# Down products of the feed-forward halves in three column blocks instead of two

## The reference

```
def swiglu(x, wi, wo):
    gate, up = jnp.split(x @ wi, 2, axis=-1)
    return (jax.nn.silu(gate) * up) @ wo
...
h = h + 0.5 * swiglu(rms_norm(h, ffn1_norm[li]), ffn1_wi[li], ffn1_wo[li])
```

## Time and profile before

| | |
|---|---|
| median of 3 runs | 1460.78 us |
| lowest and highest run | 1460.72 and 1460.96 us |
| profiled execution: span from the first to the last instruction | 1458.9 us |
| median of the runs less that span | 1.9 us |
| TensorE busy | 1452.6 us, 7822 matmuls |
| VectorE, ScalarE busy | 1002.6 and 778.5 us |

### The profile page before, as it was taken

The page is one execution under the profiler, slowest core; times in us unless marked ns, Lnnn a source line. Parts: engine busy times, 40 slices in busy tenths (PEclk is TensorE's granted clock), DMA queues, the critical chain, the costliest instruction groups (busy, mean ns, idle before and its releaser), DMA issues.

```text
span 1458.9 us, 18627 instructions
## 1 busy us (share of the span) xinstructions
PE 1452.6 (100%) x7822; PEld 1250.3 (86%) x7822; DVE 1002.6 (69%) x1216; ACT 778.5 (53%) x971; POOL 87.2 (6%) x113
## 2 busy tenths in 40 slices
PE   9999999999999999999999999999999999999999
PEld 7888888888888888888888888888888888888887
DVE  6976466787755867459877664787646987687653
ACT  6654355655534555345665544564435876465542
POOL 0000003000000000006100000000000800000000
PEclk9999999999999999999999999999999999999999
DMA  9855563556556555545455556475556543556552
GB/s 328 277 183 178 160 203 116 168 180 201 179 182 202 187 187 189 186 139 172 150 198 188 189 172 206 154 223 182 187 173 217 188 144 118 173 193 205 178 187 72
DMA packets 205620, 266.82 MB, mean 183 GB/s; under 512 B 6944, under 2 KB 148880, under 8 KB 205280
## 3 DMA queue, kind: packets, MB, share of 16 engines
q1 hardware_dynamic: 204320, 261.23, 54.5%
q0 software_dynamic: 1072, 4.35, 0.8%
q10 hardware_dynamic: 144, 0.05, 0.0%
HBM read 264.56 MB, written 1.05 MB: 182 GB/s over the span
## 4 chain that ended last, share of the span: by engine, by line
PE 96%; DVE 2%; ACT 1%; DMA 0%; issue 0%; DVEq 0%; ACTq 0%
PE ps L637 33%; PE ps L643 17%; PE ps L563 14%; PE ps L565 13%; PE ps L564 13%; PE ps L616 1%; PE ps L717 1%; PE ps L812 1%; DVE wlo L1632 1%; PE ps L750 1%; DVE d_i L2025 0%; DVE d_m L2021 0%; DMA G<-in_gains 0%; DVE d_i L2049 0%; PE ps L751 0%
## 5 line engine op out<-in xcount | busy, mean ns | idle before, releaser
L1632 DVE TENSOR_TENSOR wlo<-raw,whi 128x2048 fp32r<-128x2048 f32 (+5 forms) x275 | 567.4, 2068 | 259.0 <-ACT whi L1193 258.6
L1193 ACT CAST whi<-raw 128x2048 fp32r<-128x2048 f32 (+5 forms) x275 | 474.7, 1732 | 222.8 <-PE ps L565 218.4
L637 PE MATMUL ps<-xt,whi 128*128 128x512 f32 x2112 | 511.2, 391 | 0.5 <-DVE xt L2225 0.5
L637 PEld LDWEIGHTS ps<-xt,whi 128*128 128x128 f32 x2112 | 386.0, 188 | 74.4 <-DVE xt L2225 1.3
L643 PEld LDWEIGHTS ps<-xt,wlo 128*128 128x128 f32 x2112 | 274.0, 191 | 12.3
L643 PE MATMUL ps<-xt,wlo 128*128 128x256 f32 x2112 | 277.7, 283 | 0.0
L563 PE MATMUL ps<-whi,xt 128*128 128x512 f32 (+4 forms) x304 | 112.7, 371 | 0.0
L565 PE MATMUL ps<-whi,xt 128*128 128x512 f32 (+4 forms) x304 | 109.7, 361 | 0.0
L564 PE MATMUL ps<-wlo,xt 128*128 128x512 f32 (+4 forms) x304 | 109.5, 360 | 0.0
L563 PEld LDWEIGHTS ps<-whi,xt 128*128 128x128 f32 x304 | 57.3, 188 | 9.2 <-issue 1.0
L565 PEld LDWEIGHTS ps<-whi,xt 128*128 128x128 f32 x304 | 57.2, 188 | 8.5
(11 more groups left out here) (422 smaller groups left out, 1885.8 us busy)
## 6 DMA issues: line engine op xcount, KB each, us to landing
raw<-in_ffn_wi SPq DMA_DIRECT2D x85, 1024.0 KB, 4.9
raw<-in_ffn_wo SPq DMA_DIRECT2D x40, 1024.0 KB, 5.0
raw<-in_ffn_w_gate SPq DMA_DIRECT2D x22, 1024.0 KB, 5.1
raw<-in_ffn_w_up SPq DMA_DIRECT2D x22, 1024.0 KB, 5.2
raw<-in_ffn_w_down SPq DMA_DIRECT2D x20, 1024.0 KB, 4.9
raw<-in_w_in SPq DMA_DIRECT2D x14, 1024.0 KB, 5.1
raw<-in_even_w_in SPq DMA_DIRECT2D x6, 1024.0 KB, 5.2
raw<-in_ffn_wo SPq DMA_DIRECT2D x8, 512.0 KB, 3.8
```

What stands on the lines that cost most here:

```text
L637: return e.matmul(pair.ap[:, b, :], whi[:, v % SPLIT, 256 * j + 128 * b:256 * j + 128 * b + 128], XS[:, j, :, :].rearrange("p h t -> p (h ...
L1193: e.copy(whi[0:n, v % SPLIT, c], raw[0:n, v % RAW, c]).then_inc(s_hi.mark(*[(v, j) for j in js]), 1)
L1632: e.tensor_tensor(wlo[0:n, v % SPLIT, c], raw[0:n, v % RAW, c], whi[0:n, v % SPLIT, c].bitcast(F32), ALU.subtract).then_inc(s_lo.mark(*[(v ...
```

## The change

The 1024 columns of each down product are cut into three jobs of 342, 342 and 340 columns. Each has five blocks, of 5, 5, 4, 4 and 4 row tiles. In the slots of `raw`, `whi` and `wlo` the row tiles lie 384 columns apart (`PITCH`), and the copy and the subtraction touch only the first 342 (or 340) columns of each (`cut`). A block has five row tiles at most, so the calls of `steps` name five.

The first third is added into X when its job ends, then the second. After the second third the first 512 columns of X are complete, and the squares and the transposes of them follow in the third job, again behind three row tiles of its first block. `add_third` takes the place of `add_to_x` for these sums. ScalarE and VectorE call `unit()` 14 times instead of 11 around them. At the end of the kernel there are seven stores instead of five, and the halves of `last_steps` have 170 columns and four row tiles in place of 256 and two.

```diff
+THIRDS = [(0, 342), (342, 342), (684, 340)]
+PITCH = 384
...
-        self.d = [Job(f"{name}d{i}", down, full_blocks(FF), [(512 * i, 512)], None, (name, "ht")) for i in range(2)]
+        self.d = [Job(f"{name}d{i}", down, [(0, 5, 128), (640, 5, 128), (1280, 4, 128), (1792, 4, 128), (2304, 4, 128)],
+                      [third], None, (name, "ht")) for i, third in enumerate(THIRDS)]
+        for job in self.d:
+            job.pitch = PITCH
...
-        return o + [(d, i) for d in self.d for i in range(6)]
+        return o + [(d, i) for d in self.d for i in range(5)]
...
+        def cut(v, ap):
+
+            job = plan[v][0]
+            return ap if job.pitch == job.width else ap.rearrange("p (k n) -> p k n", n=job.pitch)[:, :, 0:job.width]
...
-                    hi_w, lo_w = (w[0:n, v % SPLIT, j * wd:(j + 1) * wd] for w in (whi, wlo))
+                    hi_w, lo_w = (w[0:n, v % SPLIT, j * pitch:j * pitch + wd] for w in (whi, wlo))
...
-                steps(d[0], 0)
-                for i in range(1, 6):
-                    steps(d[0], i)
-                give(d[0].name, s_dve["x", name, 0, 1])
+                for n in range(2):
+                    for i in range(5):
+                        steps(d[n], i)
+                    give(d[n].name, s_dve["added", name, n, 1])
...
-                    steps(d[1], 0, 0, 3)
+                    steps(d[2], 0, 0, 3)
                     turn_x(name, 0)
-                    steps(d[1], 0, 3)
-                for i in range(1, 6):
-                    steps(d[1], i)
+                    steps(d[2], 0, 3, 5)
+                for i in range(1, 5):
+                    steps(d[2], i)
...
-                e.copy(whi[0:n, v % SPLIT, c], raw[0:n, v % RAW, c]).then_inc(s_hi.mark(*[(v, j) for j in js]), 1)
+                e.copy(cut(v, whi[0:n, v % SPLIT, c]), cut(v, raw[0:n, v % RAW, c])).then_inc(s_hi.mark(*[(v, j) for j in js]), 1)
...
-                e.tensor_tensor(wlo[0:n, v % SPLIT, c], raw[0:n, v % RAW, c], whi[0:n, v % SPLIT, c].bitcast(F32),
+                e.tensor_tensor(cut(v, wlo[0:n, v % SPLIT, c]), cut(v, raw[0:n, v % RAW, c]), cut(v, whi[0:n, v % SPLIT, c]).bitcast(F32),
...
+            def add_third(f, i, squared):
+                c0, n = THIRDS[i]
+                pair = Pair(f.d[i].name)
+                if f.x != "in":
+                    q.wait_ge(*s_turn["xt", f.x, 1])
+                q.wait_ge(*s_act["sq", squared, 1, 1])
+                for tt in range(2):
+                    q.wait_ge(*s_mm[f.d[i].name, tt])
+                    xs = X[:, tt, c0:c0 + n]
+                    names = [("added", f.name, i, tt)] + ([("x", f.name, i - 1, tt)] if i else [])
+                    e.scalar_tensor_tensor(xs, pair.ap[:, tt, 0:n], RS[:, tt:tt + 1], xs, ALU.mult, ALU.add).then_inc(s_dve.mark(*names), 1)
```

More of the change, by code:

```diff
@@ L145, in __init__ @@
         self.act, self.key, self.k_off, self.at = act, key, k_off, {}
-        self.width = sum(c[1] for c in cols)
+        self.width = self.pitch = sum(c[1] for c in cols)
     def rows(self, i, j):
@@ L299, in pieces @@
                 return [(tuple(range(j, j + 4)), 128, slice(j * wd, (j + 4) * wd)) for j in (0, 4)]
-            return [(tuple(range(nk)), job.blocks[i][2], slice(0, nk * wd))]
+            return [(tuple(range(nk)), job.blocks[i][2], slice(0, nk * job.pitch))]
+        def cut(v, ap):
+            job = plan[v][0]
+            return ap if job.pitch == job.width else ap.rearrange("p (k n) -> p k n", n=job.pitch)[:, :, 0:job.width]
         def first(v, j):
@@ L480, in load @@
                     return
-                slot = raw[0:nr, v % RAW, 0:nk * job.width].rearrange("p (k n) -> p k n", k=nk)
+                slot = raw[0:nr, v % RAW, 0:nk * job.pitch].rearrange("p (k n) -> p k n", k=nk)
                 at = 0
@@ L524, in sync @@
                 load(v)
[L525 to L532, removed]
+            for i, (c0, n) in enumerate(THIRDS[0:2]):
+                for tt in range(2):
+                    q.wait_ge(*s_dve["added", "c2", i, tt])
+                    e.dma_start(out[0, 128 * tt:128 * tt + 128, c0:c0 + n], X[:, tt, c0:c0 + n]).then_inc(s_out.mark((i, tt)), 16)
+            for tt, c0, n in ((0, 0, 340), (1, 0, 170), (1, 170, 170)):
+                q.wait_ge(*s_dve["last", tt, c0])
+                c = slice(684 + c0, 684 + c0 + n)
+                e.dma_start(out[0, 128 * tt:128 * tt + 128, c], X[:, tt, c]).then_inc(s_out.mark((2, tt, c0)), 16)
+            q.wait_ge(*s_out[2, 1, 170])
         def tensor(e):
@@ L546, in give, with steps @@
                 idle.append((pair_of[name], emptied))
-            def steps(job, i, j0=0, j1=4):
+            def steps(job, i, j0=0, j1=5):
                 v = job.at[i]
@@ L551, in steps @@
                 pair = take(job.name) if i == 0 and j0 == 0 else Pair(job.name)
-                wd, end = job.width, i == len(job.blocks) - 1
+                wd, pitch, end = job.width, job.pitch, i == len(job.blocks) - 1
                 order = [(j, tt) for j in range(j0, min(j1, nk)) for tt in range(2)]
@@ L572, in last_steps @@
                 for tt, c0, n in ((0, 0, wd), (1, 0, wd // 2), (1, wd // 2, wd // 2)):
-                    o = own.ap[:, c0 // (wd // 2), 0:n] if tt else pair.ap[:, 0, :]
+                    o = own.ap[:, c0 // (wd // 2), 0:n] if tt else pair.ap[:, 0, 0:n]
                     for j in range(nk):
@@ L577, in last_steps @@
                         q.wait_ge(*s_lo[v, j])
-                        hi_w, lo_w = (w[:, v % SPLIT, j * wd + c0:j * wd + c0 + n] for w in (whi, wlo))
+                        hi_w, lo_w = (w[:, v % SPLIT, j * job.pitch + c0:j * job.pitch + c0 + n] for w in (whi, wlo))
                         h, l = (a[:, kt, 128 * tt:128 * tt + 128] for a in (job.act.hi, job.act.lo))
@@ L1296, in ffn @@
                     high_part(c)
-                for i in range(1, 6):
+                for i in range(9):
                     unit()
@@ L1303, in ffn @@
                     turn_x(name, 0)
-                for i in range(1, 6):
+                for i in range(4):
                     unit()
@@ L1781, in ffn @@
                         all_gains()
-                for i in range(1, 6):
+                for i in range(4):
                     unit()
-                add_to_x(name, 0, d[0], None, f.x, rs)
+                add_third(f, 0, rs)
+                for i in range(5):
+                    unit()
+                add_third(f, 1, rs)
                 unit()
@@ L1792, in ffn @@
                 else:
-                    add_to_x(name, 1, d[1], None, f.x, rs)
+                    add_third(f, 2, rs)
                 if f in (b1, c1):
@@ L1797, in last_add @@
             def last_add():
-                pair, own = Pair(c2.d[1].name), Pair("last")
+                pair, own = Pair(c2.d[2].name), Pair("last")
                 q.wait_ge(*s_turn["xt", c2.x, 1])
                 q.wait_ge(*s_act["sq", c2.x, 1, 1])
-                for tt, c0, n, o in ((1, None, 512, pair.ap[:, 1, :]), (0, 0, 512, pair.ap[:, 0, :]),
-                                     (1, 0, 256, own.ap[:, 0, 0:256]), (1, 256, 256, own.ap[:, 1, 0:256])):
+                for tt, c0, n, o in ((1, None, 340, pair.ap[:, 1, 0:340]), (0, 0, 340, pair.ap[:, 0, 0:340]),
+                                     (1, 0, 170, own.ap[:, 0, 0:170]), (1, 170, 170, own.ap[:, 1, 0:170])):
                     if c0 is None:
-                        q.wait_ge(*s_mm[c2.d[1].at[4], 1])
+                        q.wait_ge(*s_mm[c2.d[2].at[3], 1])
                     else:
@@ L1807, in last_add @@
                     after_mine()
-                    xs = X[:, tt, 512 + (c0 or 0):512 + (c0 or 0) + n]
-                    e.scalar_tensor_tensor(xs, o, RS[:, tt:tt + 1], xs, ALU.mult, ALU.add).then_inc(s_dve.mark(("x", "c2", 1, tt, c0)), 1)
+                    xs = X[:, tt, 684 + (c0 or 0):684 + (c0 or 0) + n]
+                    e.scalar_tensor_tensor(xs, o, RS[:, tt:tt + 1], xs, ALU.mult, ALU.add).then_inc(s_dve.mark(("last", tt, c0)), 1)
             def second_scale():
@@ L2262, in phase_done @@
             def phase_done(f):
-                q.wait_ge(*s_mm[f.d[1].at[5], 1])
+                q.wait_ge(*s_mm[f.d[2].at[4], 1])
                 q.wait_ge(*s_act["sq", f.name, 1, 1])
```

6 lines of the change are left out of this document (3 added, 3 removed).

## The result

The changed kernel takes 1475.41 us (median of 4 runs, 1475.0 to 1475.5) against 1460.85 us for the kernel before on the same chip: a ratio of 1.0099 with a 95% interval of 1.0085 to 1.0114. It is slower, as forecast, but by 14.6 us where 10.4 were forecast, and outside the range of 1469.4 to 1473.2.

What follows compares the result with a forecast made beforehand. TensorE was taken as full, its time being matmuls times spacing. Matmuls +10.4, end +0.1, last sum -0.1 gave a span of 1469.3 us; with 1.9 us from span to median, 1471.2 us, range 1469.4 to 1473.2.

Steps and rivals of the forecast that it cites:

- conversions: Copy and subtraction of each weight block in the down jobs: need 3.6 us, at least 7.5 us available, so nothing added.
- loads: Weight loads of the down jobs: five-tile block of 855 KB in shorter rows, about 12.8 us cycle against 5.0; 0.
- transposes: The 8 transposes, 0.87 us, stay behind three row tiles of the third job; 1.6 us of cover remain: 0.
- banks: Three down jobs and the transposes take the four pairs of banks in turn, with no added wait: 0.
- The narrower matmuls keep the constant: Against the rival that narrower down matmuls lose it: 144.8 ns at 342 columns, kernel 15.7 us faster, 1445.1; 2 in 100.
- an added matmul costs 13.3 and not 2.3 ns: Against the rival that each of 792 extra matmuls costs only 2.3 ns: +1.8 us, 1462.6; 3 in 100.
- no wait of TensorE in a down product was added: Against the rival that weight supply falls behind: up to 74 us, 1545, or milder, 1477; 4 in 100.
- The new widths lie between 324 and 360, so nothing is extrapolated: Down matmuls: spacing taken from measured widths, 155.8 ns for 342 columns and 155.0 for 340, +10.4 us.
- one constant for every width: Each matmul costs about 13.3 ns beyond columns/2.4, not shrinking with width; 792 more matmuls give 10.5 us.
- straight lines between rows for the bounds: Down matmuls: lines from 324 to 360 and from 256 to 512 columns give +9.5 and +10.6 us, the term's ends.
- The last 24 matmuls: Split matmuls of 170 columns at the kernel's end: 84 ns apart, +0.1 us; at the transposes' rate 145 ns, 1.5 us more.
- The last sum: Final sum at the kernel's end gets shorter, 0.39 us for 170 columns: -0.1 us.

Runs made afterwards that it cites:

- the split kernel: The kernel before with each 512-column matmul of its down jobs issued as two of 256, nothing else changed: 1481.56 us against 1460.69, ratio 1.0143.

## Why the prediction was wrong

The sign and the mechanism were right: TensorE is full, the time is its matmuls times their spacing, and nothing else becomes late. A size was wrong, the spacing at 342 columns. Every term that the forecast set to 0 (conversions, loads, transposes, banks) is 0 within what the runs can tell, and the rivals are refuted. The narrower matmuls keep the constant, an added matmul costs 13.3 and not 2.3 ns (1572 of them in the split kernel), and no wait of TensorE in a down product was added.

**The step that failed** is "The new widths lie between 324 and 360, so nothing is extrapolated" and the 155.8 ns it led to. It took one constant for every width, and straight lines between rows for the bounds. The widths between lie on no line: 338 columns cost 159.9 ns, 342 157.7, 346 159.5. Why isn't known. The two rows it went by were themselves no points of a clean line, at other pitches; 12.8 and 13.9 ns over the streaming time were read as scatter about a constant, and were signs of this. The trace before has a plainer one: in whole nanoseconds the 23 steps of the earlier trace rows run from 159 to 169, where nearly all steps of the 512 columns of the earlier trace rows are 226 or 227. That 340 columns came out at 155.2, beside the 155.0 forecast, is luck of the pitch: packed they take (21.35 - 0.87)/131 = 156.3. The bounds came from lines, so they were too narrow. The band between the neighbouring multiples of sixteen, 153.3 to 160.0, would have been the wider one: from 1584 x 2.5 ns = 4.0 us below the value taken to 1584 x 4.2 = 6.6 us above it, and it holds the measured time.

**What it cost.** 1584 matmuls at 157.7 and not 155.8 ns ((635.36 - 593.72)/264 us over both jobs): +3.0 us. At 340 columns five halves are 155.2 and not 155.0, +0.1 us, and a1 is 0.2 us shorter than the others, through the steady stretch behind its transposes. The last 24 matmuls at 110 and not 84 ns: +0.6 us. The forecast had chosen the low end of its bounds there, 84 against 145, because the row of 256 columns was nearer in kind; the measured value is near the 109 ns of the transposes' row, taken as it stands and not scaled with the width. The last sum took the 0.39 us forecast, and from the last matmul's end to the end of the span are 2.8 us where they were 2.7 us. The median stands 2.2 us above the span, not 1.9, since the profiled execution, 1475.0 us, was the shortest of the four. The sum is 3.0 + 0.1 - 0.2 + 0.6 + 0.1 + 0.1 (the last sum was forecast as a gain and the end grew) + 0.3 = 4.0 of the 4.2 us between 1471.2 and 1475.4.

The Trainium skill's gap of the columns over 2.4 plus about 2.5 ns (the page and section that the prediction names) doesn't hold for these streams: at four widths that are steady, 256, 336, 352 and 512, it is 13.3 ns. The same section calls that formula the gap of an isolated matmul, and gives about 131 ns at 512 columns for a stream in which each matmul has a load, as here; the 226.7 ns measured don't agree with that either.

## What to carry over

In a kernel whose TensorE never waits, the price of a change is its matmuls from start to start: count them, and read the spacing at the very width and pitch, since a width between two measured ones can cost as much as the next multiple of sixteen, and even one width moved by up to 4.5 ns within a kernel. Cutting a product into more column blocks adds a constant for each matmul, 13.3 ns here, and a matmul of 84 or 170 columns paid about 110 ns. If blocks must be unequal, make them multiples of sixteen with row tiles at a pitch that has been measured: 352, 336 and 336 at a pitch of 384 ran 3.3 us faster than 342, 342 and 340.

## What the runs showed that was not expected

- The start-to-start time of fp32r matmuls with a load each is the columns plus 32 at 2.4 GHz for 256 and 512 columns at a pitch of 512 and for 336 and 352 at 384: 120.0, 153.3, 160.0 and 226.7 ns, in steady steps.
- Between 336 and 352 columns, at a pitch of 384, all measured widths lie between the values of these two in no order: 159.9 ns for 338, 155.2 for 340, 157.7 for 342, 157.7 for 344, 159.5 for 346, 158.4 for 348, 160.0 for 350. The steps of 338 and 350 are steady; those of 342 repeat every six matmuls between 152 and 164 ns. Why isn't known.
- At one width and pitch the spacing can change where the stream is interrupted: 344 columns go at 153.3 ns before the transposes of c1 and at 157.8 behind them, 340 columns behind those of a1 at 153.4 and of b1 at 155.1.
- The pitch of the moving operand plays a part: 336 columns take 153.3 ns at a pitch of 384, 154.2 at 352, 154.8 at 336 and 154.7 at 400; 352 columns take 159.7 to 160.0 at pitches of 384, 352 and 400.
- Narrow matmuls with a load each came no closer than about 110 ns on average: 111 for 84 columns and 110 for 170.
